# Attention products with the values split into two column tiles of 64 query rows, in a two-block transformer kernel

## What is computed

```python
o_mem = jnp.einsum('bhsn,bnhd->bshd', p, v)               # memory, 256 keys
o     = jnp.einsum('bthk,btkd->bthd', p, v_sel)           # sparse layer, up to 512 keys
o_s   = jnp.einsum('bgtjk,bgtkd->btgjd', p_s, v_sel)      # selected branch; the window branch is alike
o     = jnp.einsum('bnkgqs,bnskd->bnqkgd', p, vb)         # sliding window of 128 in bands of 256 keys
```

## Time and profile before

| | |
|---|---|
| median of 3 runs | 2467.14 us (2463.45 to 2471.73) |
| span of the profiled execution | 2468.0 us |
| TensorE matmul, busy | 2423.7 us (98%), 11990 instructions |
| TensorE weight load, busy | 2004.0 us (81%), 11990 |
| VectorE, ScalarE, GpSimd, busy | 936.0, 1079.6, 972.3 us |

### The profile page before, as it was taken

One profiled execution on the slowest core, in us unless ns is written; L12 is line 12 of the kernel. 1 busy time (PEld: TensorE's weight loads), 2 busy tenths in 40 slices (PEclk: granted clock), 3 DMA queues, 4 the chain that ended last, 5 costly groups with the idle time before them and its releaser, 6 DMA issues.

```text
span 2468.0 us, 36248 instructions
## 1 busy us (share of the span) xinstructions
PE 2423.7 (98%) x11990; PEld 2004.0 (81%) x11990; DVE 936.0 (38%) x2051; ACT 1079.6 (44%) x1917; POOL 972.3 (39%) x484
## 2 busy tenths in 40 slices
PE   8999999999999999999999999999999999999998
PEld 6888888888778978888887978788888797788886
DVE  7976322211477753222214243321211773311212
ACT  7565443432347754444335534432332583432321
POOL 4821444444331124444443413444443423444441
PEclk9999999999999999999999999999999999999999
DMA  4300333333420013233332312233333202233331
GB/s 154 116 30 18 90 97 101 94 102 105 128 69 10 1 35 94 93 102 93 103 102 79 103 39 81 77 95 95 100 94 94 69 18 69 86 101 95 94 94 68
DMA packets 57866, 202.75 MB, mean 82 GB/s; under 512 B 7072, under 2 KB 7968, under 8 KB 57392
## 3 DMA queue, kind: packets, MB, share of 16 engines
q1 hardware_dynamic: 54864, 196.02, 26.2%
q10 hardware_dynamic: 2912, 5.55, 0.6%
HBM read 199.44 MB, written 2.10 MB: 82 GB/s over the span
## 4 chain that ended last, share of the span: by engine, by line
PE 41%; issue 14%; POOL 7%; ACT 1%; DVE 1%; POOLq 0%; DVEq 0%; ACTq 0%
PE bank L764 36%; POOL w_lo L618 7%; PE bank L1008 1%; PE bank L967 1%; PE bank L979 1%; ACT h_hi L1492 1%; PE bank L1372 0%; PE bank L1353 0%; ACT gained L1495 0%; PE bank L1367 0%; PE bank L793 0%; PE bank L1055 0%; PE bank L881 0%; PE bank L770 0%; PE bank L786 0%
## 5 line engine op out<-in xcount | busy, mean ns | idle before, releaser
L618 POOL TENSOR_TENSOR w_lo<-w_raw,w_hi 128x1024 fp32r<-128x1024 f32 x368 | 883.3, 2401 | 1197.7 <-ACT w_hi L1449 1188.1
L764 PE MATMUL bank<-h_hi,w_hi 128*128 128x512 f32 x1648 | 650.5, 395 | 7.2 <-DVE tmp L2476 2.1
L764 PE MATMUL bank<-h_lo,w_hi 128*128 128x512 f32 x1648 | 642.2, 390 | 0.0
L764 PE MATMUL bank<-h_hi,w_lo 128*128 128x512 f32 x1648 | 642.2, 390 | 0.0
L1449 ACT ACTIVATE w_hi<-w_raw 128x1024 fp32r<-128x1024 f32 x368 | 386.8, 1051 | 242.7 <-PE bank L764 214.0
L764 PEld LDWEIGHTS bank<-h_hi,w_hi 128*128 128x128 f32 x1648 | 309.8, 188 | 82.3 <-issue 5.9
L764 PEld LDWEIGHTS bank<-h_hi,w_lo 128*128 128x128 f32 x1648 | 309.7, 188 | 65.2
L764 PEld LDWEIGHTS bank<-h_lo,w_hi 128*128 128x128 f32 x1648 | 309.9, 188 | 65.0 <-issue 2.2
L764 PE MATMUL bank<-mact_hi,w_hi 128*128 128x512 f32 x512 | 199.3, 389 | 1.7 <-DVEq L2342 1.7
L764 PE MATMUL bank<-mact_hi,w_lo 128*128 128x512 f32 x512 | 199.2, 389 | 0.0
L764 PE MATMUL bank<-mact_lo,w_hi 128*128 128x512 f32 x512 | 199.2, 389 | 0.0
(11 more groups left out here) (403 smaller groups left out, 3489.3 us busy)
## 6 DMA issues: line engine op xcount, KB each, us to landing
w_raw<-in_weights SPq DMA_DIRECT2D x368, 512.0 KB, 3.6
out<-x ACTq DMA_DIRECT2D x8, 256.0 KB, 2.1
x<-in_xT SPq DMA_DIRECT2D x4, 256.0 KB, 6.8
x<-in_xT ACTq DMA_DIRECT2D x4, 256.0 KB, 7.4
memx<-in_memT SPq DMA_DIRECT2D x1, 1024.0 KB, 9.8
cmp_w1k<-in_cmp_w ACTq DMA_DIRECT2D x1, 1024.0 KB, 5.6
cmp_w1v<-in_cmp_w ACTq DMA_DIRECT2D x1, 1024.0 KB, 7.5
rope_c<-in_rope_c SPq DMA_DIRECT2D x1, 256.0 KB, 8.4
```

Source lines behind the costliest of these rows:

```text
L618: nc.gpsimd.tensor_tensor(w_lo[:, t % RING, :], w_raw[:, t % RAW, :], w_hi[:, t % RING, :].bitcast(F32), ALU.subtract).then_inc(lo_ready, 1)
L764: r = nc.tensor.matmul(out, a, b, start=first and n == 0, stop=last and n == 2)
```

## The change

Each product of `values` is made twice. The first takes query rows 0 to 63 of `probT` as its stationary operand (128 keys by 64 columns) and writes PSUM partitions 0 to 63, and the second takes rows 64 to 127 and writes partitions 64 to 127. Both have the same moving operand. The array is addressed for these products as column tiles 64 wide instead of as one tile 128 wide. The other products, the waits and the signals are as before. The compressed units return earlier in the function and keep their one product.

```diff
                         v = v_nsa[:, kt, (br - 1) * P + l * HD:(br - 1) * P + (l + 1) * HD]
-                    r = nc.tensor.matmul(output_place(kind, u, g), probT[:, g % 2, n * P:(n + 1) * P], v, start=n == 0, stop=n == len(kts) - 1)
+                    for rows in (slice(0, HD), slice(HD, P)):
+                        p = probT[:, g % 2, n * P + rows.start:n * P + rows.stop]
+                        r = nc.tensor.matmul(output_place(kind, u, g)[rows, :], p, v, start=n == 0, stop=n == len(kts) - 1)
                 r.then_inc(pv_done, 1)
```

## The result

The changed kernel takes 2477.3 us in the median against 2467.3: a ratio of 1.0038 with a 95% interval of 1.0024 to 1.0052, so it is slower by 0.38%, or 10 us. One of its five runs (2514.8 us, at a mean granted clock of 0.980 against 0.997 to 0.999 in the other four) is left out of the ratio. The forecast was 2484 (+17).

The account below looks back on a forecast made before the run. TensorE was taken to bound the kernel, its time paid almost one for one. Units outside memory added 70.9 - 52.9 = +18.0 us, memory units -0.9: +17, thus 2484 us; the case's range was 2476 to 2500, the overall range 2464 to 2556.

Parts of the forecast that it names:

- the mechanism that was forecast with 0.48: Split values on TensorE: mode changes cost more than paired short loads save, +17 us, range 2476 to 2500.
- Load of 64 columns: Values' weight loads on TensorE: half the columns take half the time, 0.056 us instead of 0.112.
- Two tiles at once: Values on TensorE: both column tiles work simultaneously, 0.112 us less per key tile, 60.0 us saved over 536.
- The way in and out: Around each unit's values: mode changes empty TensorE; first load 0.197 us later, 0.144 us before the next scores load.
- The sum at the values: Net change by stream: dsa +2.9, nsa +5.9, memory units -0.9, sliding window +9.3, total +17 us.
- tiles by turns: Rival at the values: column tiles alternate, so the 60.0 us are not saved; 2545 us, chance 0.26 including full-price loads.
- no emptying: Rival at the mode changes: column tiles need no drain, so faster, 2445 or 2422 us; chance of faster 0.13.
- TensorE's present waits of 2.1 us: TensorE's loads waiting for exponentials in nsa: might absorb a microsecond or two of added time, not counted.
- The clock: TensorE's clock should hold, since mem0 empties the array twice in every unit and has 1.00.

Follow-up runs that it names:

- one_tile: The changed kernel with both halves sent to the same column tile from each unit's second key tile on; 2506.2 us.
- tiny_col: The kernel before, values whole, plus one unread one-column product in a 64-wide column tile ahead of each unit's values; 2608.4 us, partly at half clock.
- only1: The kernel before with the split only in units with one key tile; 2473.1 us in one run.
- only4: The kernel before with the split only in units with 4 key tiles; 2462.3 us against 2466.2, ratio 0.9983.
- tiny_full: The kernel before plus one unread one-column whole-array product ahead of each unit's values; 2539.0 us, and 2487.2 us when run again.

## Why the prediction was right, and where its size was off

**The chance and the sign.** Slower by 0.38%, by the mechanism that was forecast with 0.48. The measured 2477.3 lies in that case's own range (2476 to 2500), near its lower end.

**Load of 64 columns.** Taken as 0.056 us, half of the 0.112 for 128. In the changed kernel the 384 steps between passes in nsa took 22.54 us, 0.0587 each, so the guess was 5% low. The Trainium skill's rule that the time goes with the columns ("TensorE: Matmul & The Clock Gate", "LDWEIGHTS (loading the stationary operand)") agrees with the trace, 0.0587 against 0.112 for twice the columns.

**Two tiles at once.** Read from the row tiles of linear attention, and right for column tiles: the trace has the two tiles' first loads of a unit at 822.800 and 822.807, and one_tile shows what is lost without it, 0.111 us per key tile. The sentence of the Trainium skill by which loads overlap matmuls in flight only when the row group differs ("TensorE: Matmul & The Clock Gate", "The mechanism") did not hold as it stands: all these loads have the same rows. The same section also lets a load go ahead into a background weight buffer, and no run here tells whether that is what happens. The rival "tiles by turns", 2545, is out.

**The way in and out.** Forecast: 0.197 us later in and 0.088 more until the next load on the way out (0.144 - 0.056). Measured in nsa: (29.74 - 10.72) / 96 = 0.198, and from the last load of the values to the next scores 16.41 / 80 = 0.205 against 8.93 / 80 = 0.112, 0.093 more. The price read from the row tiles carried over to the column tiles unchanged, and tiny_col shows it without any split product. What the traces show is when loads start; that 0.09 us of each way is the emptying and the rest lost cover is worked out from them. The Trainium skill's rule on changing the mode ("TensorEngine Tiling (Array Packing)", "Key Properties") agrees with both. The rival "no emptying", 2422 to 2445, is out.

**The sum at the values.** Forecast +2.9, +5.9, -0.9 and +9.3, together +17. Measured +3.6, +7.6, -1.0 and +9.2, together +19.4. The dearer loads account for that: 536 x 2 x 0.0027 = 2.9 us. By units, only1 gave +12.3 us for 52 units (counted 12.4), and only4 was a gain, -2.8 at the values (counted -2.7).

**The step that was mis-sized.** "A microsecond or two may vanish in TensorE's present waits of 2.1 us, which I don't count." It was 9.6 us at the transposes, of which about 0.9 came back in neighbouring steps. My reading of the earlier trace rows was wrong: I took the row named after ScalarE for the wait and passed over the row "issue" of 5.1 us at the same line. Both shrink together when TensorE comes later, and both end at a fixed distance from the end of an exponential, 0.05 or 0.12 us. That these are waits that can take in added time, and only so much, is shown by four kernels in dsa: 5.1 us added at the values gave S to T 1.6 us less (tiny_full), 3.6 added gave 2.7 less (the change), 2.8 added gave 1.7 less (only1), and 15.6 added gave no more than 2.6 less (tiny_col). In nsa 31.7 us added took 5.3 away and 7.6 took 5.0. Beyond that every microsecond is paid. The stretches show the same step: forecast were 3 us more in dsa, 6 in nsa and 9 in the sliding window, and they grew by 1.0, 2.9 and 7.8. The two errors of size partly cancel, 2.4 us too little at the values and 8.7 too much for leaving out what the waits take in. Had the loads cost what I took, the result would have been near 2475, just under the case's own range, so that the hit of that range owes something to luck. The sign does not.

**The clock.** The forecast said that it would hold, and in dsa and nsa it did. That the profiled execution of the kernel before had a dip in the sliding window (half clock from 1984.5 to 1991.3 us), about 2.3 us of its 59.3, I had seen as 0.94 and not priced. One more at 2039.1 us, behind the stream's last load of values, made what follows 1.2 us longer than in the changed kernel. The two are most of the 3.9 us by which the spans differ less (6.8) than the stretches (10.7).

## What to carry to other kernels

A product whose time is its weight loads can be halved by two column tiles, but each group of such products between whole-array work pays about 0.29 us here for two changes of the tiling mode and the lost cover of one load. Count the loads per group before splitting: in this kernel, outside the memory units, groups of 8 loads of 0.112 us gained (only4) and groups of 2 lost (only1). For 4 and 6 loads the counts give a loss of 0.13 and 0.03 us; no run has them alone. Added time on the bounding engine is first taken in by its own waits, so read those, the ones with no named releaser too, before pricing a small change one for one.

## What was not expected of the hardware

The second column tile joined late when its instructions stood far behind the first's: with 3 or 4 key tiles per unit the two overlapped only in part (0.66 and 0.89 us against 0.50 and 0.61), with 2 fully. What sets this reach was not tested.

TensorE's granted clock was at half for the whole sliding-window stream in one execution of tiny_full (111.2 us) and full in another execution of the same program (62.4 us), on another chip. A single profiled time of such a kernel says nothing until the clock row is read. What starts such a spell was not found.
